# First expert layer: the last two slot blocks enter the sum by 0/1 matrix products, and the norm behind it is rewritten around them

## The reference, cut to what matters

```python
# experts are computed per pair (token, expert); slots are padded per expert to blocks of 128
yb = lax.map(run, (xb, block_expert)).reshape(cap, d)     # run: (silu(x @ wg) * (x @ wu)) @ wd
y  = einsum('nkd,nk->nd', yb[slot_of_pair], gate)
h  = layer_norm(DN_ALPHA * h + y, ln_ffn_g, ln_ffn_b)
```

## Time and profile before

| | |
|---|---|
| median of 3 runs | 2617.89 us (2617.45 to 2618.25) |
| profiled execution, its time | 2618.86 us |
| its span in the profile | 2617.1 us |
| PE busy | 2428.3 us (93%) |
| DVE busy | 2029.3 us (78%) |
| ACT busy | 1703.7 us (65%) |
| POOL busy | 667.7 us (26%) |
| mean granted clock of PE | 0.963 of full speed |

### The profile page before, as it was taken

The page is one execution under the profiler, slowest core; times in us unless marked ns, Lnnn a source line. Parts: engine busy times, 40 slices in busy tenths (PEclk is TensorE's granted clock), DMA queues, the critical chain, the costliest instruction groups (busy, mean ns, idle before and its releaser), DMA issues. The chain is left out here.

```text
span 2617.1 us, 37790 instructions
## 1 busy us (share of the span) xinstructions
PE 2428.3 (93%) x12697; PEld 2084.4 (80%) x12697; DVE 2029.3 (78%) x2585; ACT 1703.7 (65%) x1814; POOL 667.7 (26%) x490
## 2 busy tenths in 40 slices
PE   8979989986988999999999599997979999999996
PEld 8969968875776888888888499996867888888885
DVE  3788876677888898898998543536778898998886
ACT  3369836765217878878877465663147878878775
POOL 0105717742001212222221412120013222222223
PEclk9999999997988999999999699998979999999998
DMA  5502334314339699989898511104259699999994
GB/s 171 139 9 89 81 100 123 87 34 135 113 124 372 232 350 368 370 338 328 297 371 297 183 57 33 41 17 164 97 190 349 240 346 368 377 371 370 379 370 153
DMA packets 114991, 564.76 MB, mean 216 GB/s; under 512 B 23351, under 2 KB 27703, under 8 KB 65616
## 3 DMA queue, kind: packets, MB, share of 16 engines
q1 hardware_dynamic: 89776, 512.19, 53.5%
q0 software_dynamic: 25120, 51.36, 7.1%
HBM read 574.25 MB, written 73.29 MB: 247 GB/s over the span
## 5 line engine op out<-in xcount | busy, mean ns | idle before, releaser
L2138 DVE TENSOR_TENSOR e0wlo<-e0raw,e0whi 128x2048 fp32r<-128x2048 f32 x214 | 486.6, 2290 | 62.4 <-ACT e0whi L1986 62.4
L1986 ACT ACTIVATE e0whi<-e0raw 128x2048 fp32r<-128x2048 f32 x214 | 409.8, 1915 | 93.5 <-PE e0u L93 39.0
L2138 DVE TENSOR_TENSOR e1wlo<-e1raw,e1whi 128x2048 fp32r<-128x2048 f32 x138 | 312.7, 2287 | 44.9 <-ACT e1whi L1986 44.8
L1986 ACT ACTIVATE e1whi<-e1raw 128x2048 fp32r<-128x2048 f32 x138 | 263.9, 1913 | 41.4 <-PE e1yp L93 20.6
L91 PE MATMUL odd_banks<-h2T_hi,odd_w_hi 128*128 128x348 f32 x480 | 171.2, 357 | 1.8 <-PEq L123 1.3
L2138 DVE TENSOR_TENSOR e_wu<-e1raw,e_wu 128x2048 fp32r<-128x2048 f32 x70 | 160.4, 2295 | 15.3 <-ACT e_wu L1986 15.1
L1986 ACT ACTIVATE e_wu<-e1raw 128x2048 fp32r<-128x2048 f32 x70 | 134.3, 1918 | 48.2 <-PE e1u L93 30.4
L92 PE MATMUL odd_banks<-h2T_lo,odd_w_hi 128*128 128x348 f32 x480 | 154.9, 323 | 0.0
L93 PE MATMUL odd_banks<-h2T_hi,odd_w_lo 128*128 128x348 f32 x480 | 154.6, 322 | 0.0
L91 PE MATMUL m_y<-m_whi,m_xhi 128*128 128x512 f32 (+1 forms) x304 | 123.4, 406 | 23.7 <-DVE m_wlo L1645 23.2
L93 PE MATMUL m_y<-m_whi,m_xlo 128*128 128x512 f32 (+1 forms) x304 | 120.4, 396 | 0.0
(11 more groups left out here) (509 smaller groups left out, 7337.1 us busy)
## 6 DMA issues: line engine op xcount, KB each, us to landing
e0raw<-in_moe_w_gate SPq DMA_DIRECT2D x72, 1024.0 KB
e0raw<-in_moe_w_up SPq DMA_DIRECT2D x72, 1024.0 KB
e0raw<-in_moe_w_down SPq DMA_DIRECT2D x72, 1024.0 KB
e1raw<-in_moe_w_gate SPq DMA_DIRECT2D x70, 1024.0 KB
e1raw<-in_moe_w_up SPq DMA_DIRECT2D x70, 1024.0 KB
e1raw<-in_moe_w_down SPq DMA_DIRECT2D x70, 1024.0 KB
qki_w_raw<-in_w_even SPq DMA_DIRECT2D x22, 512.0 KB
odd_w_raw<-in_w_odd SPq DMA_DIRECT2D x20, 512.0 KB, 3.8
```

Of the source, the lines that this page charges most:

```text
L1986: act.activation(w_hi[i], raw[:, i, :], ACT.Copy).then_inc(hi_done[i], 1)
L2138: dve.tensor_tensor(w_lo[i], raw[:, i, :], w_hi[i].bitcast(F32), ALU.subtract).then_inc(lo_done[i], 1)
```

## The change

Layer 0 takes the ending that layer 1 has. `experts` loses the `rest is None` branches: no scatter for the last two blocks, no wait for its landing; SP loads rows 0 to 3, then the gains, then rows 4 to 8, beside the last blocks; the kept results and the 0/1 matrices are made by ACT and DVE, with 16 more columns for the meta tokens. `combine` is rewritten: it adds the products to the rows, and its norm is that of `last_norm`. What differs from `last_norm`: one pair of accumulator banks instead of two, each engine's order by turn, and the transposes and projection steps behind it. `LOW_BEHIND` is 4 for ACT's `high` and DVE's `low` alike.

```diff
@@ experts, SP @@
-            if rest is None:
-                sp.wait_ge(lo_done[1], m + 3)
-                sums.load_gains(sp)
-                sp.wait_ge(y_stored, m * 16 + 32)
-                sums.load_rows(sp, BEFORE_CHANGE)
-            else:
...
+            sp.wait_ge(y_stored, m * 16)
+            for i in WU:
+                sp.wait_ge(lo_done[i], m + 2)
+            sums.load_rows(sp, BEFORE_GAINS)
+            sp.wait_ge(lo_done[1], m + 3)
+            sums.load_gains(sp)
+            sums.load_rows(sp, BEHIND_GAINS)
@@ experts, POOL @@
-            if rest is None:
...
-                scatter(m)
...
-                pool.indirect_dma_start(sum_d, bass.IndirectOffsetOnAxis(ix[:, 0:1].bitcast(U32), 0), x[:], None,
-                                        bounds_check=n_tok - 1, oob_is_err=False, compute_op=ALU.add).then_inc(y_stored, 16)
-                pool.drain()
-                pool.wait_ge(y_stored, m * 16 + 32)
-                pool.sem_inc(y_free, 1)
-            else:
-                pool.drain()
+            pool.drain()
@@ combine @@
-STEPS_BEHIND = {5: 4, 6: 4, 7: 4, 8: TILE_STEPS - 12}
+STEPS_BEHIND = {6: range(0, 4), 7: range(4, KC), 8: range(KC, 2 * KC)}
+LOW_BEHIND, TURN_BEHIND = 4, 3
...
+        acc = odd.bank[:, 0:2, :]
@@ combine, DVE @@
-            for n in range(N + 4):
+            def add(n):
+                dve.wait_ge(acc_mm, n + 1)
+                dve.wait_ge(sums.loaded[n], 16)
+                dve.tensor_tensor_reduce(x(n), flat(acc, n), x(n), 1.0, 0.0, ALU.add, ALU.add, col(n, TOTAL)).then_inc(added, 1)
+            def gain(n):
+                dve.wait_ge(mean_done, n + 1)
+                dve.wait_ge(square_done, n + 1)
+                dve.scalar_tensor_tensor(x(n), x(n), col(n, MEAN), flat(g_ps, n), ALU.subtract, ALU.mult).then_inc(gained, 1)
+                dve.wait_ge(root_done, n + 1)
+                dve.reciprocal(col(n, RSTD), col(n, STD)).then_inc(scales, 1)
+            for n in range(N + LOW_BEHIND):
                 if n < N:
-                    stats(n)
+                    add(n)
...
-                if 2 <= n <= N + 1:
-                    gain(n - 2)
-                if n >= 4:
-                    low(n - 4)
+                    gain(n - 1)
+                if n >= LOW_BEHIND:
+                    low(n - LOW_BEHIND)
@@ combine, ACT @@
-            for n in range(N + 3):
+            for n in range(N + LOW_BEHIND):
                 if n < N:
-                    root(n)
+                    square(n)
                 if 1 <= n <= N:
-                    centre(n - 1)
-                if n in (5, N):
+                    rescale(n - 1)
+                if n in (2, N):
                     odd.split_hi(act, n // N)
-                if n >= 3:
-                    high(n - 3)
+                if n >= LOW_BEHIND:
+                    high(n - LOW_BEHIND)
@@ combine, PE @@
+            def sums_of(n):
+                at, q = tok0(blocks[n]), toks(blocks[n])
+                if n:
+                    pe.wait_ge(added, n)
+                for j in range(2):
+                    for e in range(2):
+                        w = rest.place(e)[:, at:at + q]
+                        pe.matmul(acc[0:q, j, :], w, rest.y_hi(e)[:, HALVES[j]], start=e == 0, stop=False)
+                        last = pe.matmul(acc[0:q, j, :], w, rest.y_lo(e)[:, HALVES[j]], start=False, stop=e == 1)
+                last.then_inc(acc_mm, 1)
...
+            for n in range(N + TURN_BEHIND):
+                if n < N:
+                    sums_of(n)
+                if n >= TURN_BEHIND:
+                    turn(n - TURN_BEHIND)
+                    steps(STEPS_BEHIND.get(n - TURN_BEHIND, ()))
+            steps(range(2 * KC, 3 * KC)).then_inc(odd.tile_mm, 1)
```

More of the change, by code:

```diff
@@ L2395, in step, with combine @@
                    (hT_hi[:, k, m], hT_lo[:, k, m]), k == 0, k == KC - 1)
-def combine(nc, name, const, sums, out_d, hT_hi, hT_lo, beside, odd):
+def combine(nc, name, const, sums, rest, out_d, hT_hi, hT_lo, beside, odd):
     blocks, x = sums.blocks, sums.rows
@@ L2422, in _ @@
         def _(sp):
-            sums.load_rows(sp, BEHIND_CHANGE)
             beside(sp)
@@ L2474, in _, with square, rescale @@
         def _(act):
[L2475 to L2479, removed]
+            def square(n):
+                act.wait_ge(added, n + 1)
+                act.activation(junk[0:toks(blocks[n]), :], x(n), ACT.Square, scale=-float(D), bias=col(n, TOTAL), accum_out=col(n, VAR)
+                               ).then_inc(square_done, 1)
+                act.wait_ge(square_done, n + 1)
+                act.activation(col(n, STD), col(n, VAR), ACT.Sqrt, scale=float(D) ** -3, bias=eps[0:toks(blocks[n]), :]).then_inc(root_done, 1)
+            def rescale(n):
+                act.wait_ge(gained, n + 1)
                 act.wait_ge(scales, n + 1)
-                act.activation(x(n), x(n), ACT.Identity, bias=col(n, 17), scale=col(n, 16)).then_inc(centred, 1)
+                act.activation(x(n), x(n), ACT.Copy, scale=col(n, RSTD)).then_inc(scaled, 1)
             def high(n):
@@ L2520, in _, with steps @@
                 last.then_inc(t_mm, 1)
-                for i in range(sum(STEPS_BEHIND.get(m, 0) for m in range(n)), sum(STEPS_BEHIND.get(m, 0) for m in range(n + 1))):
+            def steps(part):
+                last = None
+                for i in part:
+                    if i % KC == 0:
+                        pe.wait_ge(lo_d, BLOCKS_OF[i // KC])
                     if i == 0:
                         pe.wait_ge(odd.lo_done, 1)
-                    if i % KC == 0:
-                        pe.wait_ge(lo_d, BLOCKS_OF[i // KC])
+                        pe.wait_ge(added, N)
                     if i == 2 * KC:
@@ L2528, in _ @@
                     last = odd.step(pe, 0, i, hT_hi, hT_lo)
-            last.then_inc(odd.tile_mm, 1)
+                return last
+            for n in range(N + TURN_BEHIND):
+                if n < N:
+                    sums_of(n)
[3 more added lines that the diff above has]
+            steps(range(2 * KC, 3 * KC)).then_inc(odd.tile_mm, 1)
 def last_norm(nc, name, const, sums, rest, out_d):
@@ L2927, in load_odd @@
                         sp.dma_start(wab[:], A["w_rg"]).then_inc(wab_loaded, 16)
-                    combine(nc, "c0", const, sums, h2_d, hT_hi, hT_lo, beside=load_odd, odd=odd)
+                    combine(nc, "c0", const, sums, rest, h2_d, hT_hi, hT_lo, beside=load_odd, odd=odd)
                 gate = c.sb("gate", [P, RT, TP])
```

113 lines of the change are left out of this document (45 added, 68 removed).

## The result

The changed kernel takes 2624.48 us (median of 14 runs, 2621.21 to 2628.83) beside 2618.07 us for the kernel before (14 runs, 2613.44 to 2623.37). The ratio is 1.0026 with a 95% interval of 1.0019 to 1.0034: slower by 6.8 us (5.0 to 8.9). The forecast was 2629.8, range 2623.5 to 2637.

A forecast was written before the change was run, and what follows sets the result against it. Bounds: a 13.4 us chain between stages, then a 45.0 us norm bound by DVE. Start 9.7 us earlier, norm 3.8 + 17.0 + 4.6 + 18.1 + 23.1 = 66.6 us, so end 11.9 us later: 2629.8 us, range 2623.5 to 2637.

The forecast's parts named there:

- The start: Expert stage's last product to the norm's start: 3.67 us as in layer 1, so the norm starts 9.7 us earlier.
- The ring: Norm from turn 4 on: ACT and DVE steps each wait for the one before, 6.03 us per block.
- Rival 1: Norm: the ring does not close, DVE's work sets 3.6 us turns; norm 55.9 us, kernel 2619 us; chance 0.08.
- adds 0 to 4: Norm's first four periods: one accumulator pair makes add and products take turns; 17.0 us, range 13.6 to 20.4.
- first add: Norm's beginning: waits for eight products, 3.79 us behind PE's first product, at half clock.
- add 4 to add 5: Norm's turn with the 16-token block's high and low part: 4.6 us, from 4.4 to 5.3.
- adds 5 to 8: Norm's three later turns, each set by the ring: 3 x 6.03 = 18.1 us.
- add 8 to end: Norm's tail, to PE's last projection product: 23.1 us, up to 27 with PE at half clock for about eight steps.
- margin for handovers: Whole norm: handovers of 0.03 to 0.1 us read from other places can take off or add 2 to 3 us.
- The clock: PE in adds 0 to 4: two of four periods at half clock, the attention stage being the nearest row; 17.0 us.
- Rival 2: PE stays at half clock through the whole norm: kernel 2636 to 2638 us; chance 0.13.
- Rival 3: Norm's start not gained in full, because the barrier or SP's loads come later: 2631 to 2633 us; chance 0.06.

The follow-up runs named there:

- Experiment 3: The changed kernel's expert stage and early start with the norm of the kernel before, kept results not added: 0.9964 of the kernel before, 2608.25 us.
- Experiment 1: Changed kernel with ACT's high part one turn earlier (block n-3 in turn n): 0.9997 of the kernel before, 2616.96 us.
- experiment 2: Changed kernel with ACT's high part in the same turn but ahead of the rescale: 1.0009 of the kernel before, 2619.8 us.
- experiments 4 and 8: Changed kernel with two products per block instead of eight, 2621.85 us; changed kernel with two accumulators for blocks 0 to 3, 2624.24 us.
- kernel 6: As kernels 5, with the projection steps one block earlier: 0.9996 of the kernel before, 2615.03 us.
- kernels 5: Experiment 1 with the odd weights split early, on ACT and DVE instead of POOL's low parts: 1.0004 of the kernel before, 2617.94 us.
- kernel 10: As Kernel 9, with the odd weights split later, high parts at turns 1 and 2, low at 3 and 4: 0.9987, 2612.9 us.
- Kernel 9: All edits of kernel 6 plus two accumulators for blocks 0 to 3: 0.9986 of the kernel before, 2614.74 us.

## Why the prediction was right, and where its size was off

**The start** was right: 3.52 us behind the last product (3.67 said), by the path of layer 1, and no row load released an add. Experiment 3 prices it at 9.4 us.

**The ring** was right and decided the sign: 5.95 us per turn, 6.03 said from handovers of layer 1 and of the old norm. Experiment 1 opens it (3.53), experiment 2 shortens it by one link (4.92), and experiments 4 and 8 change what PE does and leave it at 5.95. Rival 1, in which it does not close, fell with the first trace. Experiment 1 also shows what rival 1 would have given: its sum was a norm of 55.9 us and 2619, and with the ring open the norm took 54.7 and the kernel 2617. So the ring is what makes the change slower instead of even.

**The size** was off: 6.8 us measured, 11.9 said. The mis-sized term is adds 0 to 4. I had taken two of four periods at half clock, 17.0 us. The first trace of the changed kernel has 13.8, all four at full clock, and the second 15.5, one at half. Term by term, said and in the first trace:

```
first add        3.8    3.5
adds 0 to 4     17.0   13.8
add 4 to add 5   4.6    4.3
adds 5 to 8     18.1   17.9
add 8 to end    23.1   23.3
norm            66.6   62.8
```

The other terms sum to 49.6 said and 49.0 measured. With the start at 3.52 instead of 3.67 and the norm 3.8 us shorter, the forecast of +11.9 becomes the +7.9 of the trace, and that is inside the interval of the runs. The second trace gives +9.8 by the same count, so one trace is good to some 2 us here.

That the range held is in part luck. Its working gave 2626.2 with every term at its lower bound, and the measured 2624.48 lies below that; only the margin for handovers, down to 2623.5, covers it. The tail came close for a reason that the sum did not have: PE was at half clock for transpose 6 and the four steps behind it, as its upper bound of 27 us assumed, and that cost next to nothing, since transpose 7 still waited 0.20 us for a low part.

**The clock** is where the row that I leaned on misled. The attention stage in the earlier trace rows was at half clock with PE busy 3.65 of 5 us; here PE is busy less than that and holds full clock. The busy table of the changed kernel (PE, PEld, DVE, ACT, POOL, PEclk, DMA, GB/s):

```profile
1457.50:1461.00 3.50, 2.16 (x9) 1.43 (x8) 1.22 (x2) 2.10 (x3) 0.24 (x1) 1.00 1.04 425
1461.00:1464.50 3.50, 2.13 (x8) 1.43 (x8) 2.52 (x5) 2.92 (x6) 0.25 (x1) 1.00 0.17 69
1464.50:1468.00 3.50, 2.13 (x8) 1.43 (x8) 2.54 (x5) 2.62 (x5) 2.22 (x2) 1.00 0.00 0
```

The attention stage itself would have warned: 20 us ahead of the earlier trace rows PE was busy less and at full clock, and it fell from there.

```profile
590.00:595.00 5.00, 3.38 (x22) 2.76 (x23) 4.97 (x12) 2.71 (x6) 0.00 (x0) 1.00 0.01 2
...
600.00:605.00 5.00, 3.92 (x18) 3.38 (x17) 5.00 (x7) 4.75 (x12) 5.00 (x7) 0.69 0.01 3
```

So the busy share in one row does not tell the level of another stretch, and two executions of the changed kernel differ in it with the same code. What decides it here stays open. The rule of the Trainium skill, page "TensorE: Matmul & The Clock Gate", section "A second HAM failure mode: psum-queue depth-cycling", that such pauses make the clock swing, is borne out in part: in kernel 6 PE was at half clock in the first period, at full clock in the second and third and at half clock in the fourth, behind pauses of 0.51 and 1.56 us; in the changed kernel it was at half clock in none or one.

**Rival 2**, half clock throughout, did not come: the granted clock was 0.53 in the first 3.5 us and 1.00 up to 1475.6. It was low again twice, 0.52 from 1481.6 to 1484.7, behind a pause of 2.77 us and inside a turn that took 5.95 all the same, and 0.56 from 1493.5 to 1505.0. **Rival 3** fell with the start. The forecast that DVE idles about 2.4 us ahead of each low part, released by ACT's high part, is in the rows above as 2.32.

## What to carry to other kernels

When two engines in strict order each take work of several blocks in a turn, write down for every wait in which turn its releaser stands. A wait within the same turn on both sides makes a ring whose length is the sum of all links. With the same wait one turn back DVE's own work set the pace here (3.53 us instead of 5.95). That was one index, worth 7.5 us. And when such a ring is opened, look for what it hid: the next delay (POOL's weight split, then the same split on DVE beside POOL's bias, and PE's clock in the first turns) took part of the gain each time.

## What the runs showed of the hardware that I had not expected

DVE's low part of an odd weight reads two operands from SBUF. Where it met no bias of POOL it took 1.2 us; begun while a bias ran it took 2.50, and it ended 1.1 us behind the bias. (In kernels 5, 6 and 10 it took 2.52, 2.53 and 2.37 in the same situation.) Kernel 9, DVE and POOL:

```profile
1462.97 1.22 DVE L2360 TENSOR_TENSOR odd_w_lo<-odd_w_raw,odd_w_hi 128x1024 fp32r<-128x1024 f32 x1 [0.80 <-ACT odd_w_hi L2356]
...
1466.52 2.50 DVE L2360 TENSOR_TENSOR odd_w_lo<-odd_w_raw,odd_w_hi 128x1024 fp32r<-128x1024 f32 x1
```

```profile
1465.59 2.34 POOL L2484 TENSOR_TENSOR e0raw<-e0raw 16x1024 f32<-16x1024 f32 x1
```

In kernel 10 it is once the other way round: DVE's low part began first, at 1464.23, and took 1.21 us, and POOL's bias took 3.38 us instead of 2.4.

```profile
1464.30 3.38 POOL L2484 TENSOR_TENSOR e0raw<-e0raw 128x1024 f32<-128x1024 f32 x1 [0.91 <-ACT e0raw L2457]
```

So the one that begins second is held up by about what is left of the first. The Trainium skill, page "SBUF — State Buffer", section "SBUF: two separate sides", says it of a DVE instruction with two SBUF inputs against a GpSimd one that reads SBUF: they share one pair of ports, the one that starts first has it for the whole instruction, and the other "fully blocks". Both traces agree: the low part ended 1.1 us behind the bias, about its own 1.2, and the bias 2.2 us behind the low part, nearly its own 2.4. DVE's adds and low parts of the norm read PSUM and one operand of SBUF, and show no such lengthening beside the bias: in kernel 10, beside the bias that runs from 1474.42 to 1476.82, they take 1.20 and 1.21 us. I had moved the weight's low part to DVE as if it cost 1.2 us at any place.
